# Gate and up panels of a feed-forward block: one 512-column product of the high weights with both halves of the activation, in place of two 256-column products

## What is computed

```python
D_FF = 2816

def swiglu_ffn(x, w_gu, w_down):
    gate, up = jnp.split(x @ w_gu, 2, axis=-1)
    return (jax.nn.silu(gate) * up) @ w_down

for layer in range(DEPTH_2):
    g = norm_g[layer]
    h = swiglu_ffn(rms_norm(x, g[0]), ffn_w_gu[layer, 0], ffn_w_down[layer, 0])
    x = x + HALF_STEP * rms_norm(h, g[1])
    ...
    h = swiglu_ffn(rms_norm(x, g[4]), ffn_w_gu[layer, 1], ffn_w_down[layer, 1])
    x = x + HALF_STEP * rms_norm(h, g[5])
```

## Time and profile before

| | |
|---|---|
| median of 3 runs | 2969.29 us (2963.32 to 2969.39) |
| the profiled execution: its time | 2963.17 us |
| its span, first to last instruction | 2961.4 us |
| mean granted clock of TensorE, share of full speed | 0.967 |
| TensorE matmul (PE) busy | 2770.3 us, 94% |
| TensorE weight load (PEld) busy | 2604.5 us, 88% |
| VectorE (DVE) busy | 1634.4 us, 55% |
| ScalarE (ACT) busy | 1319.5 us, 45% |
| mean rate from HBM | 165 GB/s |

### The profile page before, as it was taken

One profiled execution on the slowest core, in us unless ns is written; L12 is line 12 of the kernel. 1 busy time (PEld: TensorE's weight loads), 2 busy tenths in 40 slices (PEclk: granted clock), 3 DMA queues, 4 the chain that ended last, 5 costly groups with the idle time before them and its releaser, 6 DMA issues.

```text
span 2961.4 us, 51769 instructions
## 1 busy us (share of the span) xinstructions
PE 2770.3 (94%) x22402; PEld 2604.5 (88%) x22402; DVE 1634.4 (55%) x1725; ACT 1319.5 (45%) x1560; POOL 115.0 (4%) x185
## 2 busy tenths in 40 slices
PE   4789999899998999997998999999999999997999
PEld 4669999889997999997897999999979999997898
DVE  3445588854554445458765545446555454463544
ACT  3435477643444334447323434334334344344433
POOL 0000000000000000000211000000000000000000
PEclk9889999999988999998999999999999999998999
DMA  5207599845551555553301555555535555552453
GB/s 165 72 23 238 174 346 353 295 164 187 165 167 65 193 184 173 189 179 100 129 4 46 195 187 184 188 184 174 177 126 173 189 167 189 182 178 83 150 185 128
DMA packets 377590, 492.13 MB, mean 166 GB/s; under 512 B 18872, under 2 KB 337760, under 8 KB 377408
## 3 DMA queue, kind: packets, MB, share of 16 engines
q1 hardware_dynamic: 365280, 479.23, 48.6%
q0 software_dynamic: 2192, 7.73, 0.8%
q10 hardware_dynamic: 9936, 2.47, 0.4%
HBM read 488.35 MB, written 1.05 MB: 165 GB/s over the span
## 4 chain that ended last, share of the span: by engine, by line
PE 87%; DVE 6%; ACT 4%; issue 1%; POOL 1%; ACTq 1%; DMA 0%; DVEq 0%; POOLq 0%
PE bank L321 19%; PE bank L323 19%; PE bank L322 19%; PE acc L321 7%; PE acc L322 7%; PE acc L323 7%; PE bank L2462 1%; ACT w_hi L286 1%; PE acc L569 1%; DVE X L480 1%; DVE act_lo L501 1%; ACTq L827 1%; PE bank L2439 1%; PE bank L2450 1%; PE bank L569 1%
## 5 line engine op out<-in xcount | busy, mean ns | idle before, releaser
L291 DVE TENSOR_TENSOR w_lo<-raw,w_hi 128x2048 fp32r<-128x2048 f32 x360 | 824.2, 2292 | 790.3 <-ACT w_hi L286 790.1
L321 PE MATMUL bank<-act_hi,w_hi 128*128 128x256 f32 x3592 | 1019.4, 284 | 9.8 <-DVE act_lo L2714 7.7
L323 PE MATMUL bank<-act_hi,w_lo 128*128 128x256 f32 x3592 | 1018.6, 284 | 0.0
L322 PE MATMUL bank<-act_lo,w_hi 128*128 128x256 f32 x3592 | 1018.5, 284 | 0.0
L286 ACT ACTIVATE w_hi<-raw 128x2048 fp32r<-128x2048 f32 x360 | 688.1, 1912 | 511.4 <-PE acc L323 265.5
L321 PEld LDWEIGHTS bank<-act_hi,w_hi 128*128 128x128 f32 x3592 | 691.6, 193 | 13.3 <-issue 10.5
L322 PEld LDWEIGHTS bank<-act_lo,w_hi 128*128 128x128 f32 x3592 | 691.4, 192 | 2.9
L323 PEld LDWEIGHTS bank<-act_hi,w_lo 128*128 128x128 f32 x3592 | 691.4, 192 | 0.0
L321 PE MATMUL acc<-w_hi,mix_hi 128*128 128x512 f32 x928 | 366.0, 394 | 6.8 <-DVE mix_lo L1999 5.6
L322 PE MATMUL acc<-w_lo,mix_hi 128*128 128x512 f32 x928 | 364.8, 393 | 0.0
L323 PE MATMUL acc<-w_hi,mix_lo 128*128 128x512 f32 x928 | 363.8, 392 | 0.0
(11 more groups left out here) (492 smaller groups left out, 3252.3 us busy)
## 6 DMA issues: line engine op xcount, KB each, us to landing
raw<-in_ffn_w_gu SPq DMA_DIRECT2D x176, 1024.0 KB, 5.1
raw<-in_ffn_w_down SPq DMA_DIRECT2D x88, 1024.0 KB, 4.9
raw<-in_ml_w_in SPq DMA_DIRECT2D x24, 1024.0 KB, 5.4
raw<-in_rt_w_in SPq DMA_DIRECT2D x24, 1024.0 KB, 5.2
raw<-in_w_up SPq DMA_DIRECT2D x20, 1024.0 KB, 7.3
raw<-in_w_gate SPq DMA_DIRECT2D x19, 1024.0 KB, 6.8
raw<-in_w_down SPq DMA_DIRECT2D x18, 1024.0 KB, 6.6
moe_raw<-in_w_down SPq DMA_DIRECT2D x14, 1024.0 KB, 6.6
```

The costliest lines, as they stand in the source:

```text
L291: dve.tensor_tensor(w_lo[0:rows, slot, 0:size], raw[0:rows, slot, 0:size], w_hi[0:rows, slot, 0:size].bitcast(F32), ALU.subtract).then_inc ...
L321: pe.matmul(dst, l_hi, r_hi, start=start, stop=False)
L322: pe.matmul(dst, l_hi, r_lo, start=False, stop=False)
L323: return pe.matmul(dst, l_lo, r_hi, start=False, stop=stop)
```

## The change

The two tiles `act_hi` and `act_lo` become the two halves of one tile `act_both`, so that for each k tile the 256 high and 256 low columns lie side by side. In the ten units that `pair` runs, a new function `pe_wide` takes the place of `pe_columns_T`. For each k it issues one matmul of `w_hi` with the 512 columns of `act_both` into a whole bank, and one of `w_lo` with the 256 columns of `act_hi` into the first half of that bank. The bank's first half then holds w_hi act_hi + w_lo act_hi, and its second half w_hi act_lo, the cross part. Each half m of a panel now fills a bank of its own, so a unit fills four.

To bring the halves together ScalarE copies the cross part to SBUF (`cross`, four copies of 128x256 in a unit), and VectorE adds it to the bank's first half into `gated` (`half_sum`, four additions of 128x256 in a unit). The Silu reads the sum in SBUF instead of the bank. The product with the Silu becomes two multiplications of 128x256 in SBUF. Four new semaphores order this. VectorE also waits for each of its own additions. Unit 0, the down panels, the number and the bytes of the transfers and all other blocks stay as they were.

```diff
     def units(self, n):
         self.p += 3 * n
-        self.n += 2 * n
-        self.e += 3 * n
+        self.n += 2 + 4 * (n - 1)
+        self.e += 3 + 5 * (n - 1)
+        self.silus += n - 1
...
-        act_hi = sb("act_hi", [P, KT, T], F32R)
-        act_lo = sb("act_lo", [P, KT, T], F32R)
+        act_both = sb("act_both", [P, KT, 2 * T], F32R)
+        act_hi, act_lo = act_both[:, :, 0:T], act_both[:, :, T:2 * T]
...
+        def pe_wide(pe, b, slot, m):
+
+            for k in range(KT):
+                w = slice(k * PW + m * P, k * PW + m * P + P)
+                if k == KT - 1:
+                    pe.matmul(bank[b][:, 0:T], w_lo[:, slot, w], act_hi[:, k, :], start=False, stop=False)
+                last = pe.matmul(bank[b][:, :], w_hi[:, slot, w], act_both[:, k, :], start=k == 0, stop=k == KT - 1)
+                if k < KT - 1:
+                    pe.matmul(bank[b][:, 0:T], w_lo[:, slot, w], act_hi[:, k, :], start=False, stop=False)
             return last
...
-            def pair(p, off, i, between=None):
+            def pair(p, off, u0, i, between=None):
                 for j in range(2):
-                    slot, r = (p0 + off + j) % RING, r0 + res_of(off) + j
                     pe.wait_ge(lo_made, p + (j + 1))
-                    pe.wait_ge(evacuated[r % BANKS], i + r // BANKS)
-                    pe_columns_T(pe, r % BANKS, slot).then_inc(tensor_done, 1)
+                    for m in range(2):
+                        r = r0 + 2 + 4 * u0 + 2 * j + m
+                        pe.wait_ge(evacuated[r % BANKS], 2 * i + r // BANKS)
+                        pe_wide(pe, r % BANKS, (p0 + off + j) % RING, m).then_inc(tensor_done, 1)
                     if j == 0 and between:
                         between()
...
-            def silu(u, h, off, i):
-
-                r = r0 + 2 * u
-                act.wait_ge(tensor_done, 6 * i + (e0 + off + 1))
-                act.activation(silu_out[:, h, :], bank[r % BANKS][:, :], ACT.Silu).then_inc(evacuated[r % BANKS], 1)
+            def cross(u, h, j, i):
+
+                for m in range(2):
+                    r = r0 + 2 + 4 * (u - 1) + 2 * j + m
+                    act.wait_ge(tensor_done, 10 * i + (e0 + 2 + 5 * (u - 1) + 2 * j + m + 1))
+                    act.activation(scratch[:, h, (2 * j + m) * T:(2 * j + m + 1) * T], bank[r % BANKS][:, T:2 * T],
+                                   ACT.Copy).then_inc(cross_copied, 1)
+
+            def silu(u, h, i):
+
+                act.wait_ge(gate_summed, 4 * i + (2 * c.silus + 2 * u))
+                act.activation(silu_out[:, h, :], gated[:, h, :], ACT.Silu).then_inc(silu_ready, 1)
             def cast(u, h, i):
-                r = r0 + 2 * u + 1
-                act.wait_ge(evacuated[r % BANKS], i + (r // BANKS + 1))
+                act.wait_ge(product_made, 4 * i + (2 * c.silus + 2 * u))
...
-                    silu(h + 1, (h + 1) % 2, off, i)
-                    split(off, i)
-                    split(off + 1, i)
+                    off, e = 2 + 3 * h, 2 + 5 * h
+                    cross(h + 1, (h + 1) % 2, 0, i)
+                    split(off, e + 2, i)
+                    silu(h + 1, (h + 1) % 2, i)
+                    cross(h + 1, (h + 1) % 2, 1, i)
+                    split(off + 1, e + 4, i)
                     cast(h + 1, (h + 1) % 2, i)
-                    split(off + 2, i)
-            tail = 2 + 6 * loops(c, units)
+                    split(off + 2, e + 5, i)
...
-            def gate(un, h, i, off):
-                r = r0 + 2 * un
-                b, b2 = r % BANKS, (r + 1) % BANKS
-                dve.wait_ge(evacuated[b], i + (r // BANKS + 1))
-                dve.wait_ge(tensor_done, 6 * i + (e0 + off + 2))
-                dve.tensor_tensor(gated[:, h, :], silu_out[:, h, :], bank[b2][:, :],
-                                  ALU.mult).then_inc(evacuated[b2], 1)
+            def half_sum(un, h, j, m, i):
+                r = r0 + 2 + 4 * (un - 1) + 2 * j + m
+                b = bank[r % BANKS]
+                dve.wait_ge(cross_copied, 8 * i + (4 * c.silus + 4 * (un - 1) + 2 * j + m + 1))
+                last = dve.tensor_tensor(gated[:, h, m * T:m * T + T], b[:, 0:T],
+                                         scratch[:, h, (2 * j + m) * T:(2 * j + m + 1) * T], ALU.add)
+                last.then_inc(evacuated[r % BANKS], 1)
+                dve.wait_ge(evacuated[r % BANKS], 2 * i + (r // BANKS + 1))
+
+            def gate(un, h, i):
+                for m in range(2):
+                    half_sum(un, h, 0, m, i)
+                dve.nop().then_inc(gate_summed, 2)
+
+            def product(un, h, i):
+                dve.wait_ge(silu_ready, 2 * i + (c.silus + un))
+                for m in range(2):
+                    half_sum(un, h, 1, m, i)
+                    cols = slice(m * T, m * T + T)
+                    dve.tensor_tensor(gated[:, h, cols], silu_out[:, h, cols], gated[:, h, cols],
+                                      ALU.mult).then_inc(product_made, 1)
...
+                    gate(h + 1, (h + 1) % 2, i)
                     dve_split(dve, 6 * i + q, q % RING)
-                    gate(h + 1, (h + 1) % 2, i, off)
+                    product(h + 1, (h + 1) % 2, i)
                     dve_split(dve, 6 * i + (q + 1), (q + 1) % RING)
                     low((h + 1) % 2, 2 * i + (h + 1))
                     dve_split(dve, 6 * i + (q + 2), (q + 2) % RING)
```

More of the change, by code:

```diff
@@ L232, in block_kernel @@
         first_turned = sem("first_turned")
+        gate_summed = sem("gate_summed")
+        cross_copied = sem("cross_copied")
+        silu_ready = sem("silu_ready")
+        product_made = sem("product_made")
         gain_loaded = sem("gain_loaded")
@@ L333, in pe_columns_T @@
                                          hi[:, k, :], lo[:, k, :], k == 0, k == KT - 1)
+            return last
+        def pe_wide(pe, b, slot, m):
[6 more added lines that the diff above has]
+                    pe.matmul(bank[b][:, 0:T], w_lo[:, slot, w], act_hi[:, k, :], start=False, stop=False)
             return last
@@ L676, in step @@
                 off = 2 + 3 * h
-                pair(6 * i + (p0 + off), off, i, first_turn if start else None)
+                pair(6 * i + (p0 + off), off, h, i, first_turn if start else None)
                 down(6 * i + (p0 + off + 2), off + 2, 2 * i + (c.hidden + h + 1), h, start)
@@ L686, in pe_units @@
             for un in range(1 + 2 * loops(c, units), units):
-                pair(p0 + tail, tail, 0)
+                pair(p0 + tail, tail, un - 1, 0)
                 if un < units - 1:
@@ L698, in act_units, with split @@
             p0, r0, e0 = c.p, c.n, c.e
-            def silu(u, h, off, i):
-                r = r0 + 2 * u
-                act.wait_ge(tensor_done, 6 * i + (e0 + off + 1))
-                act.activation(silu_out[:, h, :], bank[r % BANKS][:, :], ACT.Silu).then_inc(evacuated[r % BANKS], 1)
+            def cross(u, h, j, i):
[7 more added lines that the diff above has]
+                act.activation(silu_out[:, h, :], gated[:, h, :], ACT.Silu).then_inc(silu_ready, 1)
             def cast(u, h, i):
-                r = r0 + 2 * u + 1
-                act.wait_ge(evacuated[r % BANKS], i + (r // BANKS + 1))
+                act.wait_ge(product_made, 4 * i + (2 * c.silus + 2 * u))
                 act.activation(mix_hi[:, 2 * h:2 * h + 2, :].rearrange("p a b -> p (a b)"), gated[:, h, :],
                                ACT.Copy).then_inc(hi_done, 1)
-            def split(off, i):
+            def split(off, used, i):
                 q = p0 + off + RING
[L715 to L719, removed]
+                if q < TOTAL_PANELS:
+                    act_split(act, q % RING, 2 * i + loads(q), 10 * i + (e0 + used))
+            act.wait_ge(tensor_done, e0 + 1)
+            act.activation(silu_out[:, 0, :], bank[r0 % BANKS][:, :], ACT.Silu).then_inc(evacuated[r0 % BANKS], 1)
+            split(0, 1, 0)
+            split(1, 2, 0)
             act.wait_ge(first_turned, c.firsts + 1)
@@ L730, in act_units @@
-            tail = 2 + 6 * loops(c, units)
+                    split(off + 2, e + 5, i)
             for un in range(1 + 2 * loops(c, units), units):
-                silu(un, un % 2, tail, 0)
-                act_ahead(act, p0 + tail, e0 + tail)
+                off, e = 3 * un - 1, 5 * un - 3
+                cross(un, un % 2, 0, 0)
+                split(off, e + 2, 0)
+                silu(un, un % 2, 0)
+                cross(un, un % 2, 1, 0)
                 cast(un, un % 2, 0)
-                act_ahead(act, p0 + tail + 1, e0 + tail + 1)
+                split(off + 1, e + 4, 0)
@@ L756, in low @@
                                   ALU.subtract).then_inc(hidden_ready, 1)
-            gate(0, 0, 0, 0)
+            dve.wait_ge(evacuated[r0 % BANKS], r0 // BANKS + 1)
+            dve.wait_ge(tensor_done, e0 + 2)
+            dve.tensor_tensor(gated[:, 0, :], silu_out[:, 0, :], bank[(r0 + 1) % BANKS][:, :],
```

(4 more changed lines are left out.)

7 lines of the change are left out of this document (2 added, 5 removed).

## The result

The changed kernel took 2945.82 us (median of 4 runs, 2943.15 to 2955.07) against 2968.51 us for the kernel before (4 runs, 2963.32 to 2969.39). The ratio is 0.9933, with a 95% interval of 0.9908 to 0.9958. That is faster by 0.7%, inside the range of 2914 to 2957, with 2945.8 us where 2937 was named and a gain of 22.7 us where the sum gave 29.3. The profiled execution was the slowest of the four (2955.07 us), so its own time says little. What it shows stage by stage says more.

A forecast was written before the change was run, and what follows sets the result against it. TensorE's matmuls were taken to bound the kernel. Saving 32.5 us on them and adding 3.2 us of stalls gave -29.3 us, thus 2933.9 from the profiled execution or 2940.0 from the median; 2937 us was named, range 2914 to 2957.

The forecast's parts named there:

- What bounds the kernel: In a feed-forward unit of 16.98 us TensorE is busy throughout, so only the sum of its matmuls sets the time.
- The surplus of a matmul, whatever its width: In feed-forward panels each matmul pays about 0.013 to 0.015 us on top of its columns, at 256 and 512 alike.
- The cost of the new pair: In gate and up panels one 512 and one 256 column matmul cost 0.347 us, three before 0.3597; 32.5 us saved.
- Rival 2: In gate and up panels each change of matmul width costs time: 0.363 us a pair, about 2977 us; chance 8%.
- Rival 1: In gate and up panels the wide matmul keeps the surplus of two, near 0.24 us: 2957 to 2963 us; chance 12%.
- The evacuation beside TensorE: In the loop ScalarE rises to 8.3 and VectorE to about 10.5 us a unit, fitting beside TensorE at no cost.
- Rival 3: In the loop emptying banks becomes the bound, TensorE waiting 0.4 us in each of 80 units: 2964 to 2972; chance 5%.
- The stall in the last unit: In the last unit of each of 8 parts TensorE waits 0.4 us for the hidden values, 3.2 us in all.
- The sum: Over the whole kernel, -32.5 us from matmuls and +3.2 us from stalls give -29.3 us.

## Why the prediction came out as it did

- **What bounds the kernel.** Right. TensorE is busy in the whole of a unit before and after, and the length of a part followed the cost of its matmuls within 0.3 us in every run.
- **The surplus of a matmul, whatever its width.** Right: 13.3 ns for 512 columns also in the run with both products wide (0.2267 less 0.2133), and 13.3 for 256. Each matmul here has a weight load of its own, so whether the surplus belongs to the matmul or to its load no run tells. The Trainium skill, page "TensorE: Matmul & The Clock Gate", section "Back-to-back issue gap", gives the 2.5 ns for the gap of an isolated matmul, and the prediction took it for a stream. By that surplus the gain would have been 3 us. The measured interval excludes that: its end nearest to no change is a gain of 12 us.
- **The cost of the new pair.** This is the term that was mis-sized. "I take 0.347" came from settled values and from the first matmul after a change of width, whose +0.006 and -0.006 I let cancel. The rows held a warning: the first five wide ones after a change took 1.16 us, 0.026 over the settled value, of which the next narrow one gave back 0.006. In the alternation they don't cancel: the wide one costs 0.233 to 0.241 and the narrow one 0.113 to 0.120, 0.3523 together in a unit. A matmul saved is worth 7.5 ns in a unit, and 8.1 over the whole part, (175.45 + 0.39 - 173.25) / 320, in place of 12.7. That makes 20.7 us and not 32.5. The value lies in the bounds given (0.339 to 0.356). Rival 2 came nearest with the mechanism, a cost of changing widths, at the wrong price: 5 ns a pair and not 16, and in one stretch of each part none. Rival 1 had the right price for the wide matmul in the mix (0.237 on average), but the narrow one costs 0.117 there and not its 0.120, and its reason is out: with both products wide each costs 0.2267, so the surplus belongs to a matmul and not to 256 columns.
- **The evacuation beside TensorE.** Right. No wait for a bank or a `w_lo` in the loop, and with three narrow matmuls in the new banks a part grew by the stall alone (170.08 less 169.68). Rival 3 didn't occur.
- **The stall in the last unit.** Right in place and size: 0.39 us for 0.4. Halving two instructions removed it, as the chain's sum says.
- **The sum.** -20.7 + 3.1 = -17.6 us, which the parts show, where -29.3 was forecast. The medians of both comparisons fell by 22.7 and 22.9. The 17.6 us (ratio 0.994) are inside both intervals. The profiles of the repeated changed kernel and of the kernel before had a rest of 1555.7 and 1557.8 us, with 187 and 195 us at the lower clock; the first profile of the changed kernel had 1567.3 and 211. So the rest can move by over 10 us with the clock under the same program. Whether some of the other 5 us belong to the change stays open; between neighbouring parts, at full clock, nothing was gained. That the median came nearer to the forecast than the parts did is therefore not to the credit of the sum as far as the runs show.

## What to carry to other kernels

Read a matmul's price as the distance between starts, and split it into columns and surplus by two widths. If the surplus is large (here 13 ns on 107), merging products that share a stationary operand pays even where no column is saved. Try matmuls of one width behind one another: the same work in groups of sixteen was 1.4 us a part cheaper than in turn, though the whole time didn't show it beyond its noise. And look for the one place where the prefetch runs out, here the last unit. What two passes over a tile cost there was taken back here by working in halves, while moving matmuls ahead of the wait only moved the delay.

## What the runs showed of the hardware that I hadn't expected

- Matmuls of two widths in turn cost more than their settled values: 5 to 6 ns a pair for 512 and 256 columns, 11 ns for 512 and 384, and less than 1 ns in groups of sixteen. Groups of two (0.3480 us a pair) did better than groups of four (0.3500). And 512 and 256 in turn run in either of two patterns, 230 + 117 ns without any extra or a round of three pairs that averages 353.
- The settled surplus is the same at 256 and 512 columns: 13.3 ns on 106.7 and on 213.3 (120.0 and 226.7 ns from start to start).
- The granted clock fell to 0.50 for 3.41 us between parts in some kernels and not in others with the same idle time ahead of it (2.2 us of 8), alike in repeated profiles of groups of 16 and of the changed kernel, but not of groups of 2.
